# The attention values of a two-block kernel: V's high and low halves as 128 rows of one product, one PSUM bank per head, with the sums and the gate on other engines

## The reference

```python
s = jnp.einsum('bhqd,bhkd->bhqk', qb, k) * scale          # + forget terms in the second attention
p = jax.nn.softmax(jnp.where(key_pos[None, :] <= qpos[:, None], s, -jnp.inf), axis=-1)
o = jnp.einsum('bhqk,bhkd->bhqd', p.astype(v.dtype), v)
...
y_mla = (o_mla * jax.nn.silu(z_mla)) @ w_br_mla[l]
y_fox = (o_fox * jax.nn.silu(z_fox)) @ w_br_fox[l]
```

## Time and profile before

| | |
|---|---|
| median of 3 runs | 1813.12 us (1812.51 to 1813.47) |
| the profiled execution's own time | 1813.01 us |
| its span, first to last instruction | 1811.3 us |
| mean granted TensorE clock | 0.990 of full speed |
| steps 1 to 16 | 70.2 to 541.7 us of the span |

### The profile page before, as it was taken

How to read it: one execution, slowest core, us unless ns; L and a number is a source line. 1 busy time by engine, 2 the same in 40 slices (tenths; PEclk the granted TensorE clock), 3 DMA queues, 4 the chain that set the end, 5 groups by cost and what they waited for, 6 DMA issues and landing times.

```text
span 1811.3 us, 25404 instructions
## 1 busy us (share of the span) xinstructions
PE 1749.8 (97%) x8651; PEld 1459.3 (81%) x8651; DVE 926.3 (51%) x1718; ACT 769.2 (42%) x1341; POOL 367.8 (20%) x389
## 2 busy tenths in 40 slices
PE   6899999999999999889999999999999999999998
PEld 5787878999987888668878888888888788888886
DVE  4567664666564334476455555433346555555322
ACT  5567666555554223333343333322264433333222
POOL 4445356333330000220111111001003211111000
PEclk9999999999999999899999999999999999999998
DMA  4121121211213334223333333333232233333332
GB/s 120 52 55 38 54 55 49 59 52 55 59 47 93 93 94 144 76 59 99 94 93 93 93 93 93 99 119 96 93 93 70 82 105 93 93 93 98 90 97 86
DMA packets 282519, 150.12 MB, mean 83 GB/s; under 512 B 11791, under 2 KB 278034, under 8 KB 282450
## 3 DMA queue, kind: packets, MB, share of 16 engines
q1 hardware_dynamic: 281874, 148.95, 28.4%
q0 software_dynamic: 544, 0.20, 0.1%
q10 hardware_dynamic: 32, 0.07, 0.0%
HBM read 147.02 MB, written 2.16 MB: 82 GB/s over the span
## 4 chain that ended last, share of the span: by engine, by line
PE 83%; DVE 7%; ACT 5%; issue 3%; POOL 1%; SPq 1%; ACTq 0%; DMA 0%; DVEq 0%; POOLq 0%
PE ps L336 68%; PE ps L915 3%; PE ps L776 2%; PE ps L2248 2%; PE ps L753 2%; PE ps L736 1%; DVE arena_r L1232 1%; DVE ps L1189 1%; DVE arena_r L1202 1%; ACT arena_r L1070 1%; ACT tmp L983 1%; PE ps L637 1%; PE ps L743 1%; ACT w_split L296 1%; PE ps L787 1%
## 5 line engine op out<-in xcount | busy, mean ns | idle before, releaser
L336 PE MATMUL ps<-u,w_split 128*128 128x512 f32 x3888 | 927.0, 396 | 11.7 <-DVE u L1828 7.3
L336 PEld LDWEIGHTS ps<-u,w_split 128*128 128x128 f32 x3888 | 729.3, 189 | 179.6 <-issue 7.6
L307 DVE TENSOR_TENSOR w_split<-w_raw,w_split 128x1024 fp32r<-128x1024 f32 (+1 forms) x221 | 268.2, 1213 | 436.6 <-ACT w_split L296 436.6
L296 ACT CAST w_split<-w_raw 128x1024 fp32r<-128x1024 f32 (+4 forms) x321 | 288.7, 913 | 417.3 <-PE ps L336 382.6
L336 PE MATMUL ps<-arena_r,w_split 128*128 128x512 f32 x1824 | 417.3, 390 | 1.7 <-DVE arena_r L2388 1.7
L336 PEld LDWEIGHTS ps<-arena_r,w_split 128*128 128x128 f32 x1824 | 341.9, 188 | 74.1 <-DVE arena_r L2388 3.3
L307 POOL TENSOR_TENSOR w_split<-w_raw,w_split 128x1024 fp32r<-128x1024 f32 (+3 forms) x100 | 137.8, 1396 | 49.7 <-ACT w_split L296 37.2
L2168 POOL TENSOR_TENSOR tmp<-tmp 128x512 f32<-128x512 f32 x44 | 57.1, 1297 | 425.7 <-ACT tmp L2153 425.7
L983 ACT ACTIVATE tmp<-ps,stats 128x144 f32<-128x144 f32 (+3 forms) x128 | 69.3, 541 | 115.4 <-DVE stats L1189 114.5
L1677 POOL TENSOR_TENSOR tmp<-tmp 128x512 f32<-128x512 f32 x40 | 56.9, 1422 | 269.5 <-ACT tmp L1636 234.5
L915 PE MATMUL ps<-u,w_split 128*128 128x264 f32 x768 | 101.6, 285 | 0.6 <-POOL w_split L307 0.6
(11 more groups left out here) (250 smaller groups left out, 1491.0 us busy)
## 6 DMA issues: line engine op xcount, KB each, us to landing
w_raw<-in_w_in_dram SPq DMA_DIRECT2D x118, 256.0 KB, 3.1
w_raw<-in_w_ffn_gate_dram SPq DMA_DIRECT2D x88, 256.0 KB, 3.1
w_raw<-in_w_ffn_up_dram SPq DMA_DIRECT2D x88, 256.0 KB, 3.1
w_raw<-in_w_ffn_down_dram SPq DMA_DIRECT2D x64, 256.0 KB, 3.1
w_raw<-in_w_in_even_dram SPq DMA_DIRECT2D x32, 256.0 KB, 3.0
w_raw<-in_w_in_odd_dram SPq DMA_DIRECT2D x32, 256.0 KB, 3.1
w_raw<-in_w_ffn_down_dram SPq DMA_DIRECT2D x32, 192.0 KB, 2.7
w_raw<-in_w_br_mla_dram SPq DMA_DIRECT2D x16, 256.0 KB, 3.0
```

The lines of the kernel that those rows point to most:

```text
L296: ins = act.copy(dst, src)
L307: ins = dve.tensor_tensor(lo, r, hi, ALU.subtract)
L336: last = pe.matmul(out_ap, w_tile(c, ws, k - n0), moving(k, ms), start=start and n == 0, stop=stop and n == len(total) - 1, skip_group_che ...
```

## The change

- V of a pair is laid out per head and key block as 64 columns of high part beside 64 of low part. One 128-column weight tile now gives high-by-p in rows 0 to 63 and low-by-p in rows 64 to 127. With p's high and low parts as moving operand that is 2 matmuls per head and key block in place of 3 (the fourth product, low by low, is now made too).
- Head 0 goes to bank 7 and head 1 to bank 6, which the transposes use too. The meta product is two matmuls of 64 rows, one per bank.
- In the next step ScalarE copies rows 64 to 127 of both banks to SBUF (`act_lows`, behind act_exp(0)), VectorE adds rows 0 to 63 to them (`dve_sums`, behind dve_norm(0)) into `o_sum`, and GpSimd multiplies by silu(z) (`gate`, behind pool_meta(1)). In "mla" steps pool_rotate waits for the gate. transposes(0) wait for the first of the two sums, the next step's values for the second.
- `EARLY_O` is tiles 0 to 7: step 16 splits eight tiles, two behind each of act_exp(1) to act_exp(4) and of dve_norm(2) to dve_norm(5). The last pair's copies, sums and gate come in `act_mix` and `dve_mix`, ahead of tiles 8 to 15.
- The arena is laid out in another order, the zero columns and their clearing by GpSimd in the prologue fall away, and some semaphores are merged.

```diff
-VW = 3 * HD
+VW = 4 * HD
...
         def pe_transposes(pe, pr, b):
             pe.wait_ge(sem("normed"), 8 * pr + b + 1)
+            if b == 0 and not first_pair(pr):
+                pe.wait_ge(sem("o_summed"), 2 * pr - 1)
...
+            out_ = (B_O, B_T)[hh]
...
-                for n, (vs, pp) in enumerate(PASSES):
-                    pe.matmul(bank(B_O, j * P, 512), v_t[:, par, vs, j, v_cols(hh)],
-                              p_t[:, hh, pp * NQ + j, j * P:512],
-                              start=hh == 0 and j == 0 and n == 0, stop=False, skip_group_check=True)
+                for part in range(2):
+                    pe.matmul(bank(out_, j * P, 512), v_t[par][:, j, P * hh:P * hh + P],
+                              p_t[:, hh, part * NQ + j, j * P:512],
+                              start=j == 0 and part == 0, stop=False, skip_group_check=True)
             if hh == 1:
                 pe.wait_ge(sem("pm_split"), pr + 1)
-                pe.matmul(bank(B_O), v_m[0:STACK, par, :], p_m[0:STACK, 0, :], start=False, stop=True,
-                          skip_group_check=True).then_inc(sem("values"), 1)
+                for n, b in enumerate((B_O, B_T)):
+                    ins = pe.matmul(bank(b, rows=slice(0, HD)), v_m[0:STACK, par, HD * n:HD * n + HD],
+                                    p_m[0:STACK, 0, :], start=False, stop=True, skip_group_check=True)
+                ins.then_inc(sem("values"), 1)
...
+        def act_lows(act, pr):
+            act.wait_ge(sem("values"), pr + 1)
+            if not first_pair(pr):
+                act.wait_ge(sem("gated"), pr)
+            for hh, b in ((1, B_T), (0, B_O)):
+                act.copy(o_sum[HD * hh:HD * hh + HD, 0, :], bank(b, rows=slice(HD, P))).then_inc(sem("o_lows"), 1)
...
-        EARLY_O = (0, 1, 4, 5)
+        EARLY_O = tuple(range(8))
...
+                if b == 0 and not (isinstance(s, int) and s == 1):
+                    act_lows(act, s - 2)
...
-                    elif b in (2, 3):
-                        o_split_hi(act, EARLY_O[2 * b - 4:2 * b - 2])
+                    elif b in (1, 2, 3, 4):
+                        o_split_hi(act, EARLY_O[2 * b - 2:2 * b])
...
+        def dve_sums(dve, pr):
+            for n, (hh, b) in enumerate(((1, B_T), (0, B_O))):
+                dve.wait_ge(sem("o_lows"), 2 * pr + 1 + n)
+                rows = o_sum[HD * hh:HD * hh + HD, 0, :]
+                dve.tensor_tensor(rows, bank(b, rows=slice(0, HD)), rows, ALU.add).then_inc(sem("o_summed"), 1)
+
+        def gate(eng, pr, silus=PAIRS // 2 + 1):
+            eng.wait_ge(sem("z_silu"), silus)
+            eng.wait_ge(sem("o_summed"), 2 * pr + 2)
...
-                if b == 0:
-                    if not (isinstance(s, int) and s == 1):
-                        if isinstance(s, int):
-                            dve_gate(dve, s - 2, min((s - 2) // 2 + 1, PAIRS // 2 + 1))
...
                 dve_norm(dve, pr, b)
-                if gemm == "gates" and b in (3, 4):
-                    o_split_lo(dve, EARLY_O[2 * b - 6:2 * b - 4])
+                if b == 0 and not (isinstance(s, int) and s == 1):
+                    dve_sums(dve, s - 2)
+                if gemm == "gates" and b in (2, 3, 4, 5):
+                    o_split_lo(dve, EARLY_O[2 * b - 4:2 * b - 2])
...
                     if b == 2:
                         pool.wait_ge(sem("pm_copied"), 8 * pr + 2)
+                        if not (isinstance(s, int) and s == 1):
+                            pool.wait_ge(sem("gated"), s - 1)
                         pool_rotate(pool, s)
...
                 pool_meta(pool, pr, b)
+                if b == 1 and not (isinstance(s, int) and s == 1):
+                    if isinstance(s, int):
+                        gate(pool, s - 2, min((s - 2) // 2 + 1, PAIRS // 2 + 1))
...
         def act_mix(act):
-            act.wait_ge(sem("gated"), STEPS)
-            o_split_hi(act, O_ORDER[len(EARLY_O):])
+            act_lows(act, STEPS - 1)
+            o_split_hi(act, range(len(EARLY_O), 2 * PAIRS - 1))
+            o_split_hi(act, (2 * PAIRS - 1,))
```

More of the change, by code:

```diff
@@ L159, in view @@
             return v, at + n
-        q_t, at = view(ra, 0, 4, 2, SEQ)
-        k_t, at = view(ra, at, 4, 2, LEN)
-        v_t, at = view(ra, at, 2, 2, NQ, VW)
+        cq_r, at = view(ra, 0, 2, 2, SEQ)
+        ckv_r, at = view(ra, at, 2, LEN)
+        ckv_m, at = view(ra, at, 2, STACK)
+        q_p, k_p, v_t = [], [], []
+        for _ in range(2):
+            pair, at = view(ra, at, 2, 2, SEQ)
+            q_p.append(pair)
+            pair, at = view(ra, at, 2, 2, LEN)
+            k_p.append(pair)
+            tiles, at = view(ra, at, NQ, VW)
+            v_t.append(tiles)
+        q_t, k_t = ([pair[:, hh] for pair in pairs for hh in range(2)] for pairs in (q_p, k_p))
         v_m, at = view(ra, at, 2, P)
@@ L455, in act_prologue @@
                 rows = pe_rows(t)
-                ins = act.copy(k_t[rows, t, HI, :], kro[rows, 2, :])
+                ins = act.copy(k_t[t][rows, HI, :], kro[rows, 2, :])
             ins.then_inc(sem("kpe_hi"), 1)
@@ L731, in pe_scores @@
                 pe.wait_ge(sem("exped"), 8 * pr + b)
-            q_i = [q_t[rows, slot, part, i * P:(i + 1) * P] for part in range(2)]
+            q_i = [q_t[slot][rows, part, i * P:(i + 1) * P] for part in range(2)]
             if i < NQ - 1:
@@ L735, in pe_scores @@
                 for m, (qs, ks) in enumerate(PASSES):
-                    ins = pe.matmul(bank(B_S + i % 2, 0, n), q_i[qs], k_t[rows, slot, ks, 0:n], start=m == 0,
+                    ins = pe.matmul(bank(B_S + i % 2, 0, n), q_i[qs], k_t[slot][rows, ks, 0:n], start=m == 0,
                                     stop=m == 2, skip_group_check=True)
@@ L1017, in q_pieces @@
             slot, b = 2 * par, 0 if gemm == "mla" else 1
-            return [(bank(b, rows=slice(64 * hh, 64 * hh + 64)), q_t[0:HD, slot + hh]) for hh in range(2)]
+            return [(bank(b, rows=slice(64 * hh, 64 * hh + 64)), q_t[slot + hh][0:HD]) for hh in range(2)]
         def k_pieces(gemm, par):
@@ L1059, in act_rope @@
                 rows = pe_rows(hh)
-                ins = act.copy(q_t[rows, 2 * par + hh, HI, :], rot[rows, 0, :])
+                ins = act.copy(q_t[2 * par + hh][rows, HI, :], rot[rows, 0, :])
             ins.then_inc(sem("rope_hi"), 1)
@@ L1083, in act_v @@
         def act_v(act, s, c, gemm, par, kk=0, i=0):
[L1084 to L1086 removed]
+            if not (isinstance(s, int) and s < 2):
                 act.wait_ge(sem("values"), s - 1)
@@ L1101, in act_v @@
             ins.then_inc(sem("v_hi"), 1)
-        EARLY_O = (0, 1, 4, 5)
-        O_ORDER = EARLY_O + tuple(t for t in range(16) if t not in EARLY_O)
+        EARLY_O = tuple(range(8))
         def o_split_hi(act, tiles):
+            if tiles[0] >= len(EARLY_O):
+                act.wait_ge(sem("values"), STEPS)
+            else:
+                act.wait_ge(sem("values"), STEPS - 1)
             act.wait_ge(sem("gated"), max(tiles) + 1)
-            act.wait_ge(sem("scores"), 8 * (STEPS - 1))
             for t in tiles:
@@ L1525, in dve_mix @@
             dve.wait_ge(sem("w_lo"), MIX + 4)
-            o_split_lo(dve, O_ORDER[len(EARLY_O):])
+            dve_sums(dve, STEPS - 1)
+            gate(dve, STEPS - 1)
+            o_split_lo(dve, range(len(EARLY_O), 2 * PAIRS))
             def body(n, first, last):
```

73 lines of the change are left out of this document (29 added, 44 removed).

## The result

The changed kernel takes 1817.3 us (median of 13 runs, 1814.6 to 1819.5), the kernel before 1812.8 (13 runs). The medians are 4.5 us apart. The ratio, taken over all runs, is 1.003, 95% interval 1.0021 to 1.0038, which is 5.4 us slower, with 3.8 and 6.9 as the ends. The profiled execution took 1816.5 us, its span is 1814.8.

The account below looks back on a forecast made before the run. The prediction took TensorE as the bound over most of a step, with a VectorE, ScalarE, VectorE chain at a few places. Gains of 5.6 us against costs of 12.25 gave +6.6, so 1819.5 us, range 1811.0 to 1823.0.

Parts of the forecast that it names:

- rival 5: Whole kernel: the forecast itself holds, 1817 to 1822 us; chance 0.45.
- The cut on TensorE: Step ends: only head 1's share of the dropped value matmuls counts, less the second meta matmul; gain 0.40 us each.
- Rival 1: Step ends: the cut arrives whole, 1.06 us each, 1810.3 us; a mild form 1811.9; chance 0.18 together.
- Fox steps: Steps 10 to 15, and 8: idle time covers the sums before transposes(1), 0.15 us in hand; cost 0.
- Rival 4: Fox steps: cover before transposes(1) is gone, 6 x 0.5 us and more, 1822.5 to 1824; chance 0.12.
- The two starts written off: Starts of steps 6 and 9: the gain of 0.4 us is lost at each.
- MLA steps 3, 5 and 7: Copies and sums taken up by ScalarE's idle; GpSimd's rotary sum holds dve_norm(2) at the shared port; cost 0.8 us each.
- rival 2: MLA steps: no hold at the port, GpSimd's operations fall between VectorE's norms; 3.9 us less, 1815.6; chance 0.2.
- MLA steps 2, 4 and 6: Behind a silu, copies and sums cannot hide, plus 0.5 for the port; cost 1.8 us, step 6 1.7.
- Step 9: Behind the eight-tile silu, transposes(0) wait for the first sum, transposes(1) come later too; cost 1.45 us.
- Step 16: VectorE paces blocks 1 to 5; sums and two more pairs of low parts delay transposes(5); cost 3.1 us.
- Rival 3: Step 16 hides the splits: 3 us less, 1816.5; chance 0.05.

Follow-up runs that it names:

- e1: The kernel before with only the first two passes of the values, with no second bank, sums or moved gate: 1801.2 us, ratio 0.9945.
- e2: The changed kernel with the GpSimd gate on only the first 8 columns of each tile: 1812.8 us, ratio 1.0009.
- e5: The changed kernel with the whole GpSimd gate in block 5 of the step instead of block 1: 1813.1 us, ratio 1.0011.
- e3: The kernel before with every silu replaced by a plain copy, so no activation table is loaded: 1806.7 us, ratio 0.9979.
- e4: The changed kernel with every silu replaced by a plain copy, so no activation table is loaded: 1809.8 us, ratio 0.9989.
- e6: The changed kernel with four tiles of o split early in step 16 instead of eight: 1818.3 us, ratio 1.0036.

## Why the prediction was right, and where its terms were off

The forecast was 1819.5 in 1811 to 1823, slower the likeliest; it is 1817.3, in the range of rival 5 (the forecast itself, 1817 to 1822) near its low edge. By its own steps:

*The cut on TensorE.* Right, and shown: by the rows a step end gives 0.45 (forecast 0.40), and the cut by itself 0.6, not 1.3 (e1). The new idle ahead of transposes(7) came, and is 0.44 for "about 0.2"; the one ahead of head 1's values grew from 0.32 to 0.55. The Trainium skill's matmul time (VectorE: DVE Perf Modes, section on the TRN2 errata) gave 0.33 for a step end; the trace disagrees, since the eight value matmuls and the two for meta take 1.79 us where it was 2.24. Rival 1, the cut arriving whole, falls with e1.

*Fox steps.* Right, cost 0: transposes(1) don't wait there, and steps 10 to 15 are 0.46 shorter each. Rival 4 falls.

*The two starts written off.* Wrong, and small: "its start's gain of 0.4 is lost too" was said of steps 6 and 9. Step 5, which ends with the start of step 6, comes out as step 3 does (+0.80, +0.82), and step 8 is 0.39 shorter, so both starts came early. The table load sets the time of the exponential behind it, not that of the scores before it: the exponential of step 6 starts 2.02 us behind the first scores where it was 1.80, so that about half of what the scores gain does not reach it.

*MLA steps 3, 5 and 7.* The cost was too small, 0.8 + 0.45 = 1.25 for the 0.8 of the forecast. The port was there, at 0.65 (e2) for the 0.8 of the forecast, so rival 2 falls. The Trainium skill's rule (SBUF — State Buffer, section "Who interferes with whom"), that the later of the two is fully blocked, holds here too: dve_norm(2) ends at 234.97, 0.23 behind the rotary sum's end. The step that failed is "+0.3, which the old idle of ScalarE before the next exponentials takes up". It costs 0.6 (e2). Where it goes shows in e5, in which the hold is gone. Step 3, before the change (first scores at 132.53):

```profile
135.59 0.68 DVE L1211 TENSOR_TENSOR tmp<-ps,tmp 64x512 f32<-64x512 f32 x1 [0.93 <-PE ps L787]
...
136.92 0.49 ACT L983 ACTIVATE tmp<-ps,stats 128x272 f32<-128x272 f32 x1 [2.79 <-DVE stats L1189]
...
143.03 0.52 PE L753 MATMUL ps<-cst,tmp 128*128 128x128 f32 x3
```

And in e5 (first scores at 132.81):

```profile
136.48 0.68 DVE L1230 TENSOR_TENSOR tmp<-ps,tmp 64x512 f32<-64x512 f32 x1
...
137.82 0.49 ACT L991 ACTIVATE tmp<-ps,stats 128x272 f32<-128x272 f32 x1 [2.19 <-DVE stats L1208]
...
142.22 1.67 PE L795 MATMUL ps<-arena_r,w_split 128*128 128x512 f32 x6 [0.41 <-ACT big L1016]
...
143.93 0.52 PE L761 MATMUL ps<-cst,tmp 128*128 128x128 f32 x3
```

The rotation starts 3.67 us behind the first scores where it was 3.06, so the push itself is 0.6 and not 0.3. The next exponential is 0.62 late (5.01 for 4.39), and so are transposes(2) (11.12 for 10.50), and the step. ScalarE's idle time before that exponential takes up nothing, since it is a wait for dve_max(1), which stands behind the rotation in VectorE's line: 2.19 us of it are left in e5. On the way q_nope (L795) waits 0.41 for ScalarE's copy of z (0.40 and 0.45 in steps 5 and 6), inside the same 0.62. The forecast asked only whether the exponential had idle time before it, not what it was waiting for. Also, it named the wait of transposes(3), to rise from 0.99 to 1.8; that is 0.98 as before in the changed kernel, and the time is lost earlier in the step, before q_nope and, as long as the hold is there, before transposes(2). dve_norm(2) takes 0.99 for the "about 1.2" of the forecast.

*MLA steps 2, 4 and 6.* Right in kind: the silu adds 0.9 to the change's cost (e3 and e4), where the forecast had 1.0 more than for steps 3, 5 and 7. The total is 1.7 + 0.45 = 2.15 for 1.8. Of it 1.5 is the push of the rotation (e5: steps 2 and 4 at 30.77), where the forecast had "1.1 to 1.3", and 0.65 the hold, where it had 0.5.

*Step 9.* 1.15 for 1.05; transposes(0) wait 2.27 us for the 1.20 before.

*Step 16.* 2.76 for 2.7, and made as forecast: e6 gives 1.85 for the added splits (forecast 2.1 less what is in hand) and leaves 26.09 - 25.18 + 0.45 = 1.36 for the copies and sums (forecast 1.4 at dve_max(2)). Rival 3 falls; it took "3 less" for the hidden splits, which is the cost of the whole step, while the forecast's own terms for the splits are 1.2 + 0.9 = 2.1. What failed is "the eight tiles left for the mix instead of twelve give nothing back". It rested on TensorE having "no gap there before", and the gap was one product pair later, 0.96 us at 553.72. With four tiles early the changed kernel waits 1.67 in the mix, so the extra splits cost nothing in the end.

*The sum* was 6.6. By the steps it is 6.6 again (8.3, less 0.4 for step 1 and 1.3 in the mix), inside the 3.8 to 6.9 of the interval, but by errors that cancel: steps 2 to 7 were 1.8 dearer than forecast, step 8 and the fox steps 0.75 better and the mix 1.3 better. The ratio says 5.4 and the medians say 4.5; which is nearest the runs can't tell. That the total came out is in part luck.

## What to carry to other kernels

A cut on the busiest engine is worth what lies behind the last chain of other engines, here 0.45 us of 1.06 per step; count the rest as idle time. Idle time in front of an operation takes up a delay only if it doesn't come from waiting for what is delayed. A cost hides in one place and not in the next, so put the change only into the steps where its cost is hidden: from the same edit, all sixteen steps gave +5.4 us and six steps gave a kernel 0.25% faster than before. When an operation is given to GpSimd, look at which operation it pushes onto which VectorE operation, not at its own time: the gate itself met nothing.

## What the runs showed of the hardware that was not expected

The held VectorE operation pays the whole of GpSimd's remainder: dve_norm of 400 columns took 0.43, 0.99 and 2.22 us, free, beside a 64-row sum of 1.27 us, and beside a split of 2.40. In both cases it ends 0.2 us behind GpSimd's operation (234.97 and 234.74 in step 6 of the changed kernel, 539.91 and 539.69 in step 16 of e5).

Behind the longest new idle times TensorE's granted clock fell, windows of the changed kernel (columns: window, length, busy time and count of PE, PEld, DVE, ACT, POOL, granted clock, DMA share, GB/s):

```profile
324.00:326.00 2.00, 1.94 (x7) 1.78 (x8) 1.92 (x6) 0.80 (x1) 1.12 (x1) 0.62 0.00 0
326.00:328.00 2.00, 2.00 (x8) 1.52 (x7) 1.32 (x6) 0.73 (x3) 1.57 (x3) 0.53 0.01 4
...
528.00:530.00 2.00, 1.91 (x11) 1.78 (x12) 1.63 (x4) 1.61 (x5) 1.30 (x2) 0.82 0.85 242
530.00:532.00 2.00, 2.00 (x8) 1.39 (x7) 1.39 (x6) 1.01 (x3) 0.00 (x0) 0.50 0.01 2
```

The first stretch follows 2.27 us of idle before transposes(0) of step 9, the second 1.79 us before transposes(1) of step 16; in the windows at 0.53 and 0.50 the engine is near its lower level of 1.2 GHz. It comes and goes from profile to profile with the same idle: in e5 the same 2.27 us is followed by this window.

```profile
321.00:323.00 2.00, 2.00 (x10) 1.53 (x10) 1.92 (x6) 0.64 (x1) 1.28 (x1) 1.00 0.00 0
```

And it cost nothing. In e5, at the full clock, TensorE gets to the next products 1.2 us earlier in the step (9.54 for 10.77 us behind its first scores) and stands there for w_split:

```profile
324.15 1.00 PE L923 MATMUL ps<-u,w_split 128*128 128x264 f32 x6 [1.01 <-POOL w_split L314]
```

Transposes(1) follow at 11.69 and 11.70 us, and step 9 takes 32.57 us in e5 and 32.56 in the changed kernel. In step 16 transposes(3) start 14.06 us behind the first scores in e5, at the full clock, and 14.05 in the changed kernel. A lower clock in the profile is a loss only where TensorE is what is waited for.
